# Two transformer blocks on one core: the matmul operands moved to different places modulo 512 bytes

## What is computed

```
first:   x = x + rmsnorm(mix(rmsnorm(x)) @ w_out);  x = x + rmsnorm((silu(h @ wg) * (h @ wu)) @ w_ffn_out)
second:  x = x + 0.5 * swiglu(x);  x = x + (gates * branches(rmsnorm(x) @ w_in)) @ w_out;  x = x + 0.5 * swiglu(x)
swiglu:  (silu(h @ w1[:, :2816]) * (h @ w1[:, 2816:])) @ w2
```

## Time and profile before

| | |
|---|---|
| Median of 3 runs | 3499.57 us (3498.72 to 3500.31) |
| The profiled execution, its own time | 3499.69 us |
| Its span | 3497.9 us |
| TensorE busy | 3395.6 us (97%), 19557 matmuls |
| VectorE busy | 2465.5 us (70%) |
| ScalarE busy | 1615.9 us (46%) |
| GpSimd busy | 55.9 us (2%) |
| DMA | 318.95 MB, mean 91 GB/s |

### The profile page before, as it was taken

The page is one execution under the profiler, slowest core; times in us unless marked ns, Lnnn a source line. Parts: engine busy times, 40 slices in busy tenths (PEclk is TensorE's granted clock), DMA queues, the critical chain, the costliest instruction groups (busy, mean ns, idle before and its releaser), DMA issues.

```text
span 3497.9 us, 49474 instructions
## 1 busy us (share of the span) xinstructions
PE 3395.6 (97%) x19557; PEld 2915.5 (83%) x19557; DVE 2465.5 (70%) x3512; ACT 1615.9 (46%) x2387; POOL 55.9 (2%) x84
## 2 busy tenths in 40 slices
PE   7999999999999999999999999999999989999999
PEld 5678988668998799887678899889988757788997
DVE  8668854759882887557895688558864888658863
ACT  4545543455562456335623355435542552335542
POOL 1000000000000000000000000000000000000000
PEclk9999999999999999999999999999999999999999
DMA  4123333212332233332132223323333213322332
GB/s 140 53 69 97 98 97 109 81 49 85 97 109 98 78 108 104 99 101 68 49 96 86 95 97 109 100 93 97 109 103 96 75 43 90 91 96 85 109 103 85
DMA packets 339643, 318.95 MB, mean 91 GB/s; under 512 B 31769, under 2 KB 312165, under 8 KB 339429
## 3 DMA queue, kind: packets, MB, share of 16 engines
q1 hardware_dynamic: 335588, 307.95, 27.8%
q0 software_dynamic: 2048, 6.16, 0.5%
q10 hardware_dynamic: 1792, 1.88, 0.2%
HBM read 313.84 MB, written 2.10 MB: 90 GB/s over the span
## 4 chain that ended last, share of the span: by engine, by line
PE 80%; DVE 14%; ACT 3%; issue 2%; SPq 0%; DMA 0%; POOL 0%; DVEq 0%; POOLq 0%
PE products L793 30%; PE products L934 25%; PE products L832 6%; PE small L832 6%; PE small L934 4%; PE products L1195 2%; DVE w_lo L2148 2%; DVE seven_x L2400 1%; PE products L1392 1%; DVE conv L2935 1%; DVE X L2168 1%; DVE x_sums L2389 1%; ACT w_hi L1518 1%; PE small L1269 1%; DVE mla_prob L2595 1%
## 5 line engine op out<-in xcount | busy, mean ns | idle before, releaser
L2148 DVE TENSOR_TENSOR w_lo<-raw,w_hi 128x2048 fp32r<-128x2048 f32 x190 | 435.2, 2290 | 483.9 <-ACT w_hi L1518 483.6
L1518 ACT ACTIVATE w_hi<-raw 128x2048 fp32r<-128x2048 f32 x190 | 363.8, 1915 | 832.7 <-PE products L793 579.5
L793 PE MATMUL products<-a_hi,w_hi 128*128 128x512 f32 (+1 forms) x1216 | 491.0, 404 | 12.7 <-DVE a_lo L2208 10.0
L934 PE MATMUL products<-seven_x,w_hi 128*128 128x256 f32 x2592 | 477.6, 284 | 7.3 <-DVE w_lo L2429 3.2
L793 PE MATMUL products<-a_hi,w_lo 128*128 128x512 f32 (+1 forms) x1216 | 476.9, 392 | 0.0
L793 PE MATMUL products<-a_lo,w_hi 128*128 128x512 f32 (+1 forms) x1216 | 476.4, 392 | 0.0
L934 PEld LDWEIGHTS products<-seven_x,w_hi 128*128 128x128 f32 x2592 | 404.5, 192 | 11.0 <-DVE w_lo L2429 4.4
L934 PE MATMUL products<-seven_x,more_hi 128*128 128x256 f32 x1632 | 382.6, 283 | 2.6 <-ACT rs_b L1627 2.6
L934 PE MATMUL products<-seven_x,w_lo 128*128 128x256 f32 x1296 | 366.7, 283 | 0.0
L793 PEld LDWEIGHTS products<-a_hi,w_hi 128*128 128x128 f32 (+1 forms) x1216 | 229.8, 189 | 69.8 <-issue 16.7
L934 PEld LDWEIGHTS products<-seven_x,more_hi 128*128 128x128 f32 x1632 | 283.8, 192 | 3.6 <-ACT rs_b L1627 3.6
(11 more groups left out here) (463 smaller groups left out, 7249.7 us busy)
## 6 DMA issues: line engine op xcount, KB each, us to landing
raw<-in_ffn_w SPq DMA_DIRECT2D x244, 512.0 KB, 4.2
raw<-in_w_in SPq DMA_DIRECT2D x108, 512.0 KB, 4.6
raw<-in_w_ffn_in SPq DMA_DIRECT2D x88, 512.0 KB, 4.2
raw<-in_w_ffn_out SPq DMA_DIRECT2D x40, 512.0 KB, 4.3
raw<-in_w_out SPq DMA_DIRECT2D x32, 512.0 KB, 4.0
raw<-in_ffn_w SPq DMA_DIRECT2D x24, 384.0 KB, 3.5
raw<-in_w_mem_kv SPq DMA_DIRECT2D x8, 512.0 KB, 3.9
raw<-in_lru_w_out SPq DMA_DIRECT2D x8, 512.0 KB, 3.4
```

The lines of the kernel that those rows point to most:

```text
L793: mm = pe.matmul(G[pair][0:m, into + b, 0:n], w[:, s, at:at + m], x, start=(first or into > 0) and k == 0 and q == 0, stop=(last or ends) ...
L934: mm = pe.matmul(out, ww[:, cut], xx[:, part], start=starts and k == 0 and q == 0, stop=name in ("P2", "P3", "P4") and k == 3 and q == 2, ...
L1518: act.activation(w_hi[:, s, :], raw[:, s, :], ACT.Copy).then_inc(hi_ready, 1)
L2148: dve.tensor_tensor(w_lo[:, s, :], raw[:, s, :], w_hi[:, s, :].bitcast(F32), ALU.subtract).then_inc(lo_ready, 1)
```

## The change

Tiles get places with different remainders modulo 512 bytes. `start_at(r)` moves the next free byte on to remainder r; `b_start_at(r)` does it in region B; `shifted(name, shape, by)` reserves 8 floats more and hands out the tile `by` bytes behind its start. `raw`, `w_hi`, `w_lo` stay at 0. The new remainders: `w_sums` 0 (unmoved), `a_hi` 64, `a_lo` 128, `h_hi` and `seven_x` 96, `h_lo` 256, `late_hi` 448, `more_hi` 352, `more_lo` 416, `early_hi` and `early_lo` 96, `yc_hi` and `yc_lo` 96, `ya_hi` 4, `ya_lo` 8, `yb_hi` 24, `yb_lo` 16, `mg_hi` 12, `mg_lo` 32. The tiles that lie over the same bytes (`ab`, `h_full`, `x_sums`, `more_sums` and so on) move with them. GpSimd's DMA scratch is set to 8192 bytes, half of what it was. No instruction is added, removed or reordered.

```diff
@@ -256,6 +256,10 @@
     base = -(-nc.sbuf_base // 64) * 64
     top = [base]
 
+    def start_at(residue):
+
+        top[0] = -(-(top[0] - residue) // LINE) * LINE + residue
+
     def place(name, shape, dt=F32, at=None):
         size = 4 * int(np.prod(shape[1:]))
         offset = top[0] if at is None else at
@@ -291,35 +295,43 @@
     w_hi = place("w_hi", [P, 2, UNIT], F32R)
     W_LO = top[0]
     w_lo = place("w_lo", [P, 2, UNIT], F32R)
+    start_at(64)
     w_sums = place("w_sums", [P, 2, UNIT], at=W_LO)
     ROWS_4 = 10 * P
     mla_prob = [place(f"mla_prob{i}", [P, ROWS_4], at=at)
                 for i, at in enumerate((W_LO + 4 * UNIT, W_HI + 4 * UNIT, BROADCASTS, BROADCASTS + 4 * ROWS_4))]
     REGION_A = top[0]
     a_hi = place("a_hi", [P, DC, SEQ], F32R)
+    start_at(128)
+    A_LO = top[0]
     a_lo = place("a_lo", [P, DC, SEQ], F32R)
+    top[0] += LINE
+    start_at(96)
     dft = place("dft", [P, TC // 2, 2, SEQ], at=REGION_A)
-    ab = place("ab", [P, TC, SEQ], at=REGION_A + 16 * KB)
+    ab = place("ab", [P, TC, SEQ], at=A_LO)
     rows = place("rows", [P, n_param_tiles, P], at=REGION_A)
     out_tok = place("out_tok", [P, TC, D], at=REGION_A)
     REGION_B = top[0]
     h_hi = place("h_hi", [P, FC, SEQ], F32R)
+    start_at(256)
+    H_LO = top[0]
     h_lo = place("h_lo", [P, FC, SEQ], F32R)
+    top[0] += 10 * LINE
     x_tok = place("x_tok", [P, TC, D], at=REGION_B)
     y_tok = place("y_tok", [P, TC, D], at=REGION_B)
 
     HALF = SEQ // 2
     QUAD = 4 * P
     seven_x = place("seven_x", [P, 11, 4 * HALF], F32R, at=REGION_B)
-    late_hi = place("late_hi", [P, 3, 4 * HALF], F32R, at=REGION_A + 20 * KB)
-    more_hi = place("more_hi", [P, 5, QUAD], F32R, at=REGION_A)
-    more_lo = place("more_lo", [P, 5, QUAD], F32R, at=REGION_A + 10 * KB)
-    early_hi = place("early_hi", [P, 3, QUAD], F32R, at=REGION_B + 76 * KB)
-    early_lo = place("early_lo", [P, 3, QUAD], F32R, at=REGION_B + 82 * KB)
-    more_sums = place("more_sums", [P, 5, QUAD], at=REGION_A + 10 * KB)
-    early_sums = place("early_sums", [P, 3, QUAD], at=REGION_B + 82 * KB)
+    late_hi = place("late_hi", [P, 3, 4 * HALF], F32R, at=REGION_A + 20 * KB + 384)
+    more_hi = place("more_hi", [P, 5, QUAD], F32R, at=REGION_A + 288)
+    more_lo = place("more_lo", [P, 5, QUAD], F32R, at=REGION_A + 10 * KB + 352)
+    early_hi = place("early_hi", [P, 3, QUAD], F32R, at=REGION_B + 76 * KB + 512)
+    early_lo = place("early_lo", [P, 3, QUAD], F32R, at=REGION_B + 82 * KB + 512)
+    more_sums = place("more_sums", [P, 5, QUAD], at=REGION_A + 10 * KB + 352)
+    early_sums = place("early_sums", [P, 3, QUAD], at=REGION_B + 82 * KB + 512)
     x_sums = place("x_sums", [P, 11, 4 * HALF], at=REGION_B)
-    h_full = place("h_full", [P, FC, SEQ], at=REGION_B + 44 * KB)
+    h_full = place("h_full", [P, FC, SEQ], at=H_LO)
     X_SUMS = {"B11": 1, "T3": 3, "T2": 5, "B12": 6, "T4": 7, "B21": 8, "T1": 9, "B22": 10}
     X_FORMS = {"B11": (seven_x[:, 0, :], seven_x[:, 1, :]), "T3": (seven_x[:, 2, :], seven_x[:, 3, :]),
                "T2": (seven_x[:, 4, :], seven_x[:, 5, :]), "T4": (seven_x[:, 6, :], seven_x[:, 7, :]),
@@ -404,13 +416,28 @@
     prob = in_b("prob", [P, 2, 4, 3 * P])
     third_prob = in_b("third_prob", [P, 4, 2 * P])
 
+    def b_start_at(residue):
+
+        b1[0] = -(-(b1[0] - residue) // LINE) * LINE + residue
+
+    def shifted(name, shape, by, at=None):
+
+        n = int(np.prod(shape[1:]))
+        flat = in_b(name, [P, n + 8], F32R) if at is None else place(name, [P, n + 8], F32R, at=at)
+        return flat[:, by // 4:by // 4 + n].rearrange("p (c n) -> p c n", c=shape[1])
+
     b1[0] = REGION_B
     yc_hi = in_b("yc_hi", [P, LC, SEQ], F32R)
     yc_lo = in_b("yc_lo", [P, LC, SEQ], F32R)
-    ya_hi = in_b("ya_hi", [P, LC, SEQ], F32R)
-    ya_lo = in_b("ya_lo", [P, LC, SEQ], F32R)
-    yb_hi = in_b("yb_hi", [P, LC, SEQ], F32R)
-    yb_lo = in_b("yb_lo", [P, LC, SEQ], F32R)
+    b_start_at(0)
+    ya_hi = shifted("ya_hi", [P, LC, SEQ], 4)
+    b_start_at(0)
+    ya_lo = shifted("ya_lo", [P, LC, SEQ], 8)
+    b_start_at(0)
+    yb_hi = shifted("yb_hi", [P, LC, SEQ], 24)
+    b_start_at(0)
+    yb_lo = shifted("yb_lo", [P, LC, SEQ], 16)
+    b_start_at(0)
     REGION_T = b1[0]
     gelu = in_b("gelu", [P, LC, SEQ])
     xa = in_b("xa", [P, LC, SEQ])
@@ -419,18 +446,18 @@
     glu = place("glu", [P, LC, SEQ], at=REGION_B)
     conv = place("conv", [P, LC, SEQ], at=REGION_B + 8 * KB)
     craw_sq = place("craw_sq", [P, 5, SEQ], at=REGION_T)
-    lru_tmp = place("lru_tmp", [P, 3, SEQ], at=REGION_B + 26 * KB)
-    craw = place("craw", [P, 6, SEQ], at=REGION_B + 32 * KB)
-    gate_w = place("gate_w", [P, LC, 2, P], at=REGION_B + 44 * KB)
-    mla_prob.append(place("mla_prob4", [P, ROWS_4], at=REGION_B + 34 * KB))
+    lru_tmp = place("lru_tmp", [P, 3, SEQ], at=REGION_B + 26 * KB + 1056)
+    craw = place("craw", [P, 6, SEQ], at=REGION_B + 32 * KB + 1056)
+    gate_w = place("gate_w", [P, LC, 2, P], at=REGION_B + 44 * KB + 1056)
+    mla_prob.append(place("mla_prob4", [P, ROWS_4], at=REGION_B + 34 * KB + 1056))
     mla_prob.append(place("mla_prob5", [P, ROWS_4], at=REGION_T))
     prob_of = [mla_prob[i] for i in (0, 1, 4, 2, 3, 0, 5, 2)]
     q_head = place("q_head", [P, MLA_HEADS, SEQ], at=REGION_T)
     kv_head = place("kv_head", [P, MLA_HEADS, SEQ], at=REGION_T + 16 * KB)
-    v_head = place("v_head", [P, TC, MLA_HEADS * HEAD], at=REGION_T + 32 * KB)
-    mg_hi = place("mg_hi", [P, DC, SEQ], F32R, at=REGION_T)
-    mg_lo = place("mg_lo", [P, DC, SEQ], F32R, at=REGION_T + 16 * KB)
-    partial = place("partial", [P, DC, SEQ], at=REGION_T + 16 * KB)
+    v_head = place("v_head", [P, TC, MLA_HEADS * HEAD], at=REGION_T + 32 * KB + 512)
+    mg_hi = shifted("mg_hi", [P, DC, SEQ], 12, at=REGION_T)
+    mg_lo = place("mg_lo", [P, DC, SEQ], F32R, at=REGION_T + 16 * KB + 32)
+    partial = place("partial", [P, DC, SEQ], at=REGION_T + 16 * KB + 32)
 
     def place_of(r):
 
@@ -3345,7 +3372,7 @@
     import concourse.bacc as _bacc
     from concourse.bass_utils import run_bass_kernel_spmd as _run
 
-    nc = _bacc.Bacc("TRN2", target_bir_lowering=False, num_devices=1)
+    nc = _bacc.Bacc("TRN2", target_bir_lowering=False, num_devices=1, dynamic_dma_scratch_size=8192)
     arrays, t = {}, {}
     for name in _INS:
         arrays[f"in_{name}"] = np.ascontiguousarray(inputs[name])
```

## The result

| | before | after |
|---|---|---|
| Median, 4 runs each | 3499.94 us (3498.72 to 3500.68) | 3521.17 us (3519.65 to 3523.77) |
| Ratio | | 1.0062, 95% interval 1.0044 to 1.0079 |
| Span of the profiled execution | 3497.9 us | 3519.2 us |
| TensorE busy | 3395.6 us | 3427.0 us |

The change costs 21.2 us. The forecast was slower, +27 us.

A forecast was written before the change was run, and what follows sets the result against it. The prediction took TensorE's matmuls to bound the kernel, each costing its columns plus about 13.2 ns. It added +45 - 18 = +27 us to 3499.69 us, forecasting 3527 us, with an 8-in-10 range of 3315 to 3600 us.

The forecast's parts named there:

- The total, +27 us: Whole kernel: 512-column loss of 45 us less 256-column gain of 18 us, giving 3527 us.
- The 512-column matmuls, +45 us: Lines 793 and 832: 8160 matmuls never fall in step, 231.9 ns for 226.4; bounds -83 to +111 us.
- the prediction's own sign: Different distances at lines 793 and 832 would say the loaded block's own place counts, not the relation.
- The 48 matmuls of the earlier trace: Two pieces with 160-float weight rows, blocks at 0, 128, 256, 384: 231.9 ns each, 5.5 ns more than equal places.
- The 256-column matmuls, -18 us: Line 934: 9072 matmuls out of step at 118.0 ns for 120.0; bounds -94 to +123 us.
- the walk-in of the earlier trace: Start of a 256-column stretch before the change: 118.0 ns at first against 120.0 later, read as not yet in step.
- VectorE, ScalarE, DMA, scratch, each 0: Other engines' moved operands, x_tok's transfers at the start and GpSimd's smaller scratch were each forecast to cost 0.
- That the clash goes: Rival: other remainders free stream and load from hitting the same bank, -177 us, 3323 us; chance 0.20.
- That only the narrow stream wins: Rival: 512-column matmuls fall in step again, 256-column ones stay out, -18 us, 3482 us; chance 0.20.
- That nothing changes: Rival: any start falls in step after ten matmuls, perhaps at any fixed relation, 3500 us; chance 0.14.
- Slower by more: Rival: loaded blocks that straddle a multiple of 512 cost each time, +100 to +234 us; chance 0.08.
- The picture of two levels, in step and out of step: TensorE's two readers: 13.2 ns over the columns in step; out of step 18.4 at 512 columns, 11.3 at 256.

The follow-up runs named there:

- e2: Kernel after the change with the operands of the seven-product stage back on multiples of 512, so only 512-column operands keep new places: 3530.92 us, ratio 1.0086.
- p2_grid: Matmul-only probe, not a kernel change: eight stream by eight block places in 32-byte steps, both widths; no distance under 226.7 ns (512 columns) or 113.3 ns (256).
- e6: Kernel before the change with all activations and sums (regions A and B) moved 64 bytes on, weights left at 0: 3488.28 us, ratio 0.9961.
- e5: Kernel before the change with all activations and sums (regions A and B) moved 256 bytes on, weights left at 0: 3499.60 us, ratio 0.9994.
- e1: Kernel before the change with every large operand, weights too, moved 64 bytes on, so all relations stay: 3501.64 us, ratio 1.0001.
- p1_places: Matmul-only probe, not a kernel change: chosen stream/block places, 64 counted matmuls each; 226.7 ns at 0/0 with 512 columns, 120.0 ns with 256.
- e3: Kernel before the change with only the operands of the seven-product stage at their new places, all others at multiples of 512: 3494.69 us, ratio 0.9982.
- e8: Kernel before the change with only the streams of the seven-product stage and x_sums at 448, smaller scratch making room: 3454.79 us, ratio 0.9877.
- e7: Kernel before the change with only GpSimd's DMA scratch halved to 8192 bytes: 3500.59 us, ratio 1.0001.
- p3_entry: Matmul-only probe, not a kernel change: the same pairs entered from different preceding pairs; stream 64, block 0 at 256 columns took 113.3 or 117.8 ns.
- e9: Kernel before the change with streams and sums of the seven-product stage at 64, weights and all others at 0: 3467.09 us, ratio 0.9909.
- e4: Kernel before the change with only seven_x and late_hi (x_sums along) at 64, every block at 0, smaller scratch making room: 3466.36 us, ratio 0.9890.

## Why the prediction was right

*What bounds the kernel.* Right: no other engine's time changed, and the three matmul shapes make +29.0 of TensorE's +31.4 us.

*The total, +27 us.* Measured +21.2. That it comes so near is in part luck. By the steady distances the wide term was 8 us too dear and the narrow one won 10 us too much, which nearly cancel, and 10 us of TensorE's longer time fell into what had been its waits, which the sum didn't have.

*The 512-column matmuls, +45 us.* What was forecast happened, unequal places cost, but the size was a fifth too large: +37 us by the steady distances, +35.3 us by the sums, 4.3 ns each instead of 5.5, and +30.0 us by itself (e2). At `piece` the distance after was met, 232.1 ns against 231.9. The value before was too low: 226.4 ns is a stretch in step, while the mean of 227.2 has the starts out of step of the earlier trace rows in it. At `by_tokens` the distance after is 230.2 ns and not 231.9.

Single pairs of p2_grid don't carry over one by one where the relation changes from matmul to matmul. `a_hi` past weights is relation 64, 228.9 ns in p2_grid and 229.2 in e6, where all streams have it; in the kernel after, between matmuls with `a_lo`, a start that streams `a_hi` is followed after 231 to 233 ns. `h_lo` at 256, as good as no move by itself (e5), has 228.3 ns there for 226.4 before. Averaged over a line's matmuls the table gives 230.8 ns for `piece` (without `ya`, `yb` and `mg_hi`, whose places it lacks) and 232.0 for `by_tokens`, measured are 232.1 and 230.2. So it gives the sum, 36 us of 37, and not the split. By the prediction's own sign, two distances that differ between the lines would mean that the block's own place counts. e1 rules that out at 64; why `by_tokens` is the cheaper one stays open.

The 48 matmuls of the earlier trace rows are also not all evidence of places. The second 24 load 96 columns, and p1_places has 230.0 ns for these at equal places. The first 24, (1623.79 - 1618.22) / 24 = 232.1 ns, carry the argument alone.

*The 256-column matmuls, -18 us.* Right in sign, a third of the size: -6.3 us in the sum per line, -6.3 in e3, -8 by the steady distances. The step that failed is the row it was taken from: the walk-in of the earlier trace rows, at equal places, stood in for the relations of the change. Nor was it a sure reading: ten distances from starts given to 0.01 us are good to 1 ns, and the gain read off them was 2 ns. p2_grid has the relations. `seven_x` past weights is relation 96, 120.1 ns, no gain, and 2592 + 1296 + 432 = 4320 of the 9072 matmuls are of that kind; so is `late_hi` past `more_hi`. `seven_x` past `more_hi` is relation 0. Only `late_hi` past weights and `seven_x` past `more_lo` have relation 192. Averaged over all, the table gives 118.9 ns, measured is 119.1. Had this term been right about what can be won, it would have been larger: e8 took 46 us from it.

*VectorE, ScalarE, DMA, scratch, each 0.* Right. The convolution is at 729 ns on average within the 711 to 747 of the earlier trace rows, ScalarE's busy time rose by 0.8 us, `x_tok` lands in 8.8 us against 8.6. The scratch was measured alone (e7). How single ScalarE operations stand was not looked into.

*The rivals.* That the clash goes: no pair of the full table comes near 216 ns at 512 columns, none is under 226.7. The 215.8 and 109.2 ns that the prediction takes from TensorE: Matmul & The Clock Gate, section Back-to-back issue gap, in the Trainium skill, are that section's formula for a single matmul; for loads and matmuls in turn it doesn't give them, so it doesn't say that 185 us could be removed. That only the narrow stream wins: not in this change, but e8 shows that it is to be had by design, at more than twice the 18 us that the rival gave. That nothing changes: out by e2, and its reason, that any fixed relation falls in step, by p1_places, where the stream at 64 stays at 233.5 ns for 64 matmuls; no change is seen where the relation is kept (e1, e5). Slower by more, since blocks straddle a multiple of 512: out by e1. The picture of two levels, in step and out of step, was too simple: p3_entry shows two steady distances for one unequal pair, and at 256 columns equal places are among the dearest.

SBUF — State Buffer, section "SBUF: two separate sides", in the Trainium skill, has TensorE's ports wait for no one. By that rule e1 and e2 would be alike. They differ by 29 us with only places changed, so the rule doesn't hold for what TensorE meets here. That it is its two readers that meet is a picture that fits and isn't shown.

*Left open.* Why equal places cost 13.3 ns and others more or less; why the distances come in steps of about 3.3 ns (113.3, 116.7, 120.0; 226.7, 230.0, 233.3); and what chooses between the two distances of a pair: in p3_entry the stream 64 bytes before its block falls into 113.3 ns much more surely than 64 behind it, in e6 and e9 the latter does too. The runs show these facts, not their cause. Nor was a version tried with both widths at their best and blocks of sums at a place of their own.

## What to carry to other kernels

Where TensorE is the bound, read start distances, not durations, and ask what each matmul costs over its columns. For float32r matmuls with a load each, the best that these runs have is stream and block at equal places modulo 256 at 512 columns (226.7 ns), and the stream 64 bytes before its block at 256 (113.3 ns); spreading the operands over places of their own lost at the first and won little at the second. Measure the table of pairs in a small kernel before moving a layout, and enter each pair by several ways, since one sample may show the rarer distance. Where relations alternate, time the real mix.

## What was unexpected in the hardware

- The distance depends on stream minus block modulo 256: 226.7 to 234.3 ns at 512 columns, 113.3 to 120.1 ns at 256 (p2_grid, steps of 32 bytes), and moving both by 64 changes nothing (e1: ratio 1.0001).
- A place 4 bytes off cost even when equal: 239.4 ns at 4/4 against 226.7 at 64/64 (p1_places, one stretch).
- One pair has two steady distances, 113.3 and 117.8 ns at 256 columns, each held for nearly all 64 matmuls of a stretch; at 512 columns stream 64 past block 0 has 233.5 (p1_places) and 229.2 (p3_entry). In the whole kernel the 256-column pair is at 118 ns in e4's trace and at 113 in e9's.
- Fewer columns in the loaded block don't make a matmul cheaper: 231.6 ns with 32, 226.7 with 128, though the load itself takes 108 ns and not 188.
